# Sums over cached values with the values streamed: four heads in four 32-column parts of the array

## The reference, cut to what matters

```
def dilated_attn_decode(q, k_all, v_all, buf_len, dil, n_back):
    ...
    s = einsum('bshe,bsjhe->bhsj', q, kg) * ATT_SCALE
    p, lse = masked_softmax_lse(s, valid[None, None])
    o = einsum('bhsj,bsjhe->bshe', p, vg)         # sum over 129 places j
...
att = einsum('blhg,blhge->blhe', softmax(lses), outs)   # the three window groups merged
```

## Time and profile before

| what | value |
|---|---|
| median of 3 runs | 2080.9 us (2079.73 to 2081.86) |
| the profiled execution | 2077.44 us |
| its span, first to last instruction | 2075.6 us |
| PE busy | 2065.5 us (100%) |
| PEld busy | 2051.1 us (99%) |
| DVE busy | 1354.1 us (65%) |
| ACT busy | 1013.0 us (49%) |
| POOL busy | 478.0 us (23%) |
| granted TensorE clock | 9 or more tenths in all 40 slices |

### The profile page before, as it was taken

How to read it: one execution, slowest core, us unless ns; L and a number is a source line. 1 busy time by engine, 2 the same in 40 slices (tenths; PEclk the granted TensorE clock), 3 DMA queues, 4 the chain that set the end, 5 groups by cost and what they waited for, 6 DMA issues and landing times.

```text
span 2075.6 us, 48725 instructions
## 1 busy us (share of the span) xinstructions
PE 2065.5 (100%) x19202; PEld 2051.1 (99%) x19202; DVE 1354.1 (65%) x1441; ACT 1013.0 (49%) x1285; POOL 478.0 (23%) x526
## 2 busy tenths in 40 slices
PE   9999999999999999999999999999999999999999
PEld 9999999999999999999999999999999999999999
DVE  7567567775556767776759978665555555555555
ACT  6654344444444545653556675554443444434443
POOL 0686424420000206764307630110000000000000
PEclk9999999999999999999999999999999999999999
DMA  8987789987887788769969886578887888778874
GB/s 253 281 270 228 262 262 279 275 258 262 260 261 221 235 297 277 235 194 328 310 197 303 276 249 196 191 249 271 269 258 245 258 265 278 250 244 259 264 218 159
DMA packets 442478, 526.45 MB, mean 254 GB/s; under 512 B 41521, under 2 KB 423393, under 8 KB 439553
## 3 DMA queue, kind: packets, MB, share of 16 engines
q1 hardware_dynamic: 427184, 507.59, 77.8%
q0 software_dynamic: 3248, 11.62, 1.6%
q10 hardware_dynamic: 11936, 5.72, 1.1%
HBM read 506.75 MB, written 105.04 MB: 295 GB/s over the span
## 4 chain that ended last, share of the span: by engine, by line
PE 94%; DVE 2%; DMA 1%; issue 1%; ACT 1%; POOL 0%; SPq 0%; DVEq 0%; ACTq 0%; POOLq 0%
PE pa L1547 30%; PE pa L1548 30%; PE pa L1552 30%; DMA raw<-in_w_in 1%; DVE w_lo L1075 1%; ACT vu L892 0%; PE pb L1750 0%; DMA yt_v<-y_dram 0%; PE pb L1810 0%; PE pb L1788 0%; PE pb L1768 0%; DVE d_tmp L1353 0%; PE pb L1617 0%; PE pa L1904 0%; SPq L555 0%
## 5 line engine op out<-in xcount | busy, mean ns | idle before, releaser
L1075 DVE TENSOR_TENSOR w_lo<-raw,w_hi 128x1024 fp32r<-128x1024 f32 x735 | 939.3, 1291 | 508.0 <-ACT w_hi L660 503.5
L660 ACT ACTIVATE w_hi<-raw 128x1024 fp32r<-128x1024 f32 x735 | 766.4, 1053 | 647.2 <-PE pa L1552 548.3
L1547 PE MATMUL pa<-xg_hi,w_hi 128*128 128x264 f32 x3960 | 924.4, 278 | 0.0
L1548 PE MATMUL pa<-xg_lo,w_hi 128*128 128x264 f32 x3960 | 916.2, 276 | 0.0
L1547 PEld LDWEIGHTS pa<-xg_hi,w_hi 128*128 128x128 f32 x3960 | 748.4, 189 | 6.9 <-issue 4.8
L1548 PEld LDWEIGHTS pa<-xg_lo,w_hi 128*128 128x128 f32 x3960 | 748.6, 189 | 0.2
L1552 PE MATMUL pa<-xg_hi,w_lo 128*128 128x264 f32 x3960 | 526.4, 276 | 0.0
L1552 PEld LDWEIGHTS pa<-xg_hi,w_lo 128*128 128x128 f32 x3960 | 483.4, 189 | 0.0
L1547 PE MATMUL pa<-act_hi,w_hi 128*128 128x264 f32 x1632 | 378.4, 276 | 0.0
L1548 PE MATMUL pa<-act_lo,w_hi 128*128 128x264 f32 x1632 | 377.9, 276 | 0.0
L1548 PEld LDWEIGHTS pa<-act_lo,w_hi 128*128 128x128 f32 x1632 | 308.5, 189 | 0.0
(11 more groups left out here) (360 smaller groups left out, 1409.5 us busy)
## 6 DMA issues: line engine op xcount, KB each, us to landing
raw<-in_ffn_w_up SPq DMA_DIRECT2D x172, 512.0 KB, 5.5
raw<-in_ffn_w_gate SPq DMA_DIRECT2D x171, 512.0 KB, 4.9
out_kv_s<-in_cache_kv_w SPq DMA_DIRECT2D x165, 512.0 KB
raw<-in_ffn_w_down SPq DMA_DIRECT2D x160, 512.0 KB, 4.6
raw<-in_w_in SPq DMA_DIRECT2D x152, 512.0 KB, 5.5
raw<-in_w_out SPq DMA_DIRECT2D x32, 512.0 KB, 4.6
raw<-in_w_ssm_branch SPq DMA_DIRECT2D x16, 512.0 KB, 4.6
raw<-in_ffn_w_down SPq DMA_DIRECT2D x16, 384.0 KB, 4.0
```

The costliest lines, as they stand in the source:

```text
L660: act.activation(w_hi[:, slot], raw[:, slot], ACT.Copy).then_inc(hi_ready, 1)
L1075: dve.tensor_tensor(w_lo[:, slot], raw[:, slot], w_hi[:, slot].bitcast(f32), ALU.subtract).then_inc(lo_ready, 1)
L1547: pe.matmul(out, wh, in_order(hi), start=first, stop=False)
L1548: pe.matmul(out, wh, in_order(lo), start=False, stop=False)
```

## The change

The values now stream, and a small matrix stands as weights. `pick` holds, for each sample k, a block of 32 columns in which only column k is one. With it as weights, the product of a head's values (128 places x 128 features) comes out as 32 rows of 128 features, of which row k is the sum and the rest zero. The four heads go to the four 32-column parts of the array, so to four groups of 32 partitions of one PSUM tile. DVE adds these tiles over the samples into `v_acc` (128 x 128, in SBUF), PE turns `v_acc` once at the end (`turn_values`), and DVE adds the part of the new row for all samples at once (`values_out`). Because the sums moved from `pb` bank 0 to bank 2, which `y_products` also writes, the waits move too: `y_products(k)` waits for `add_values(k)`, and `value_sums(k)` waits for `read_y(k - 1)`. At the end `att_hi` waits for `values_out`, and `att_lo` moves from slab 5 to slab 7.

```
-    PV = YD + 2 * YW
+    PV = YS + 2 * YW
+    PT = PV + HD
...
-                        act.wait_ge(pv_read, NS)
+                        act.wait_ge(pv_read, NS + 1)
                         act.activation(halves(att_hi[:])[:, :, :, H1], by_parity(att_v[:, :, NT:T]), ACT.Copy).then_inc(att_hi_ready, 1)
...
+                    dstep(dve.memset(pick[:], 0.0))
+                    dstep(dve.memset(pick[:].rearrange("p s r -> p (s r)")[:, 0:32 * NS:33], 1.0))
...
             def add_values(k):
                 dve.wait_ge(pv_done, k + 1)
-                dve.tensor_tensor(att_v[:, :, bass.ds(NT + k, 1)], pb[:, 0, PV:PV + NSLOT, None],
-                                  att_new[:, 0, bass.ds(NSLOT * k, NSLOT), None], ALU.add).then_inc(pv_read, 1)
+                if below(k, 1):
+                    dve.tensor_copy(v_acc[:], pb[:, 2, PV:PV + HD]).then_inc(pv_read, 1)
+                else:
+                    dve.wait_ge(pv_read, k)
+                    dve.tensor_tensor(v_acc[:], v_acc[:], pb[:, 2, PV:PV + HD], ALU.add).then_inc(pv_read, 1)
+
+            def values_out():
+                dve.wait_ge(pv_done, NS + 1)
+                dve.tensor_tensor(att_v[:, :, NT:T], pb[:, 2, PT:PT + P].rearrange("p (h b) -> p h b", b=32)[:, :, 0:NS],
+                                  att_new[:, 0].rearrange("p (b h) -> p h b", h=NSLOT), ALU.add).then_inc(pv_read, 1)
...
-                if last:                                   # in state_turn_back, slab 5
-                    dve.wait_ge(att_hi_ready, 3)
-                    dve.tensor_tensor(halves(att_lo[:])[:, :, :, H1], ...).then_inc(att_lo_ready, 1)
...
+                    if at_end and j == 6:
+                        values_out()
+                    if at_end and j == 7:
+                        dve.wait_ge(att_hi_ready, 3)
+                        dve.tensor_tensor(halves(att_lo[:])[:, :, :, H1], ...).then_inc(att_lo_ready, 1)
...
             def y_products(k):
+                pe.wait_ge(pv_read, k + 1 if k < NS - 1 else NS + 1)
...
             def state_products(k):
-                    pe.wait_ge(pv_read, k)
...
             def value_sums(k):
                 pe.wait_ge(v_sum_ready, k + 1)
-                pe.wait_ge(sv_ready, 2 * k + 2)
+                if k:
+                    pe.wait_ge(y_read, k)
+                    pe.wait_ge(pv_read, k)
                 for hh in range(NSLOT):
-                    ins = pe.matmul(pb[:, 0, PV + hh:PV + hh + 1], vu[3 * (k % 2)][:, hh * HD:(hh + 1) * HD], ones[:, 0:1],
+                    ins = pe.matmul(pb[32 * hh:32 * hh + 32, 2, PV:PV + HD], pick[:, k, :], vu[3 * (k % 2)][:, hh * HD:(hh + 1) * HD],
                                     start=True, stop=True)
                 ins.then_inc(pv_done, 1)
+
+            def turn_values():                             # PE, last iteration, after slab 6
+                pe.wait_ge(pv_read, NS)
+                pe.transpose(pb[:, 2, PT:PT + P], v_acc[:], ident[:]).then_inc(pv_done, 1)
```

More of the change, by code:

```diff
@@ L248, in build_layer @@
     head_sd = tile("head_sd", [P, T], f32, RQ)
+    pick, v_acc = tiles(RQ, 8 * T, ("pick", [P, NS, 32]), ("v_acc", [P, HD]))
     head_r = tile("head_r", [P, 2, T], f32, RT + 24 * T)
@@ L1361, in state_turn_in, with state_turn_back @@
                 dve.tensor_tensor_scan(z_out[:, 0], M, z_in[:, 0], 0.0, ALU.mult, ALU.add).then_inc(scan_ready, 1)
-            def state_turn_back(k, h, last):
+            def state_turn_back(k, h):
                 E = tab[h][:, E0:M0].rearrange("p (a c) -> p a c", a=2)
@@ L1368, in state_turn_back @@
                 dve.tensor_tensor(d_tmp[:, 1], z_out[:, 1], E[:, 0], ALU.mult).then_inc(zi_step, 1)
-                if last:
-                    dve.wait_ge(att_hi_ready, 3)
-                    dve.tensor_tensor(halves(att_lo[:])[:, :, :, H1], by_parity(att_v[:, :, NT:T]),
-                                      halves(att_hi[:].bitcast(f32))[:, :, :, H1], ALU.subtract).then_inc(att_lo_ready, 1)
                 dve.wait_ge(zi_step, 5 * k + 5)
@@ L1389, in gates_b @@
                         state_turn_in(k, j // 4)
-                    last = at_end and j == 5
-                    if last:
+                    if at_end and j == 5:
                         add_values(NS - 1)
                     if j in ((2, 6) if opening else (1, 5)):
-                        state_turn_back(2 * i + j // 4, j // 4, last)
-                    if j in ((2, 6) if opening else (2, 5)) and not last:
+                        state_turn_back(2 * i + j // 4, j // 4)
+                    if j in ((2, 6) if opening else (2, 5)) and not (at_end and j == 5):
                         add_values(2 * i + j // 4)
+                    if at_end and j == 6:
+                        values_out()
+                    if at_end and j == 7:
+                        dve.wait_ge(att_hi_ready, 3)
+                        dve.tensor_tensor(halves(att_lo[:])[:, :, :, H1], by_parity(att_v[:, :, NT:T]),
+                                          halves(att_hi[:].bitcast(f32))[:, :, :, H1], ALU.subtract).then_inc(att_lo_ready, 1)
                     if opening and j == 0:
@@ L1893, in gates_b @@
                         value_sums(2 * i + j // 4)
+                    if i == ph.iters - 1 and j == 6:
+                        turn_values()
                     if j in ((1, 5) if i == 0 else (0, 4)):
```

2 lines of the change are left out of this document (1 added, 1 removed).

## The result

The changed kernel took 2084.05 us in the median (22 runs, 2080.97 to 2088.3), the kernel before 2079.73 us (22 runs on the same chip): ratio 1.0018, 95% interval 1.0013 to 1.0024. The forecast was 2083.9 us. Against these medians the change costs 4.3 us (2.7 to 5.0 by the interval of the ratio), where the forecast reckoned 3.0 on a median of before that was 1.2 us higher. The sign, the place and the order of size are as forecast; the terms are not all right.

What follows compares the result with a forecast made beforehand. In gates_b DVE and PE were both taken as full, each waiting for the other. 4.45 us at the end, less 1.0 and 0.85 given back, plus 0.3 before, made 3.0 on 2080.9: 2083.9 us, range 2079.8 to 2087.3.

Steps and rivals of the forecast that it cites:

- Value sums on PE: PE's value-sum block in gates_b: 0.90 to 0.55 us a sample, a gain of 2.8 us in all.
- Additions: DVE's add_values in gates_b: 0.28 us for 0.15, so 0.12 us more each, 1.0 us in all.
- Waits for bank 2: y_products and value_sums in gates_b: no gain up to slab 5 of the last iteration, 0.3 us lost on DVE's chain.
- DVE goes on without a gap: Reason given in gates_b, from 65.28 of 66 us busy, that PE can't get ahead of DVE.
- The wait before `y_products(6)`: In gates_b: the wait for add_values(6), 0.41 us, moves from state_products to y_products(6), whose 0.55 us no longer lies before it.
- The end: From add_values(7) through values_out, att_hi and att_lo: PE starts attn_branch at 1199.0, 4.45 us late, standing 3.6 us.
- Given back: Behind attn_branch's start: the later waits for L1475 (1.0 us) and for zs_lo (0.85 us) fall away.
- The sum: Whole kernel: 4.45 - 1.0 - 0.85 = 2.6 us, and 0.3 for DVE's chain before, in round 3.0 us slower.
- DVE moves with PE: Rival in gates_b: DVE looks full because PE and ACT pace it; -0.1 us, 2080.8 us, chance 0.15.
- Hidden end: Rival at slabs 5 to 7, last iteration: DVE reaches add_values(7) some 4.5 us earlier against PE; 2078.3 us, chance 0.04.
- Parts in series: Rival in the value sums: the four column parts run one after another, block 1.35 us; 2086.5 us, chance 0.08.
- The clock: Rival at the end of gates_b: PE's clock falls after its stalls, costing 3.3 us; 2087.2 us, chance 0.11.

Runs made afterwards that it cites:

- e10: The changed kernel with DVE's additions for samples 1 to 7 reading 4 columns in place of 128; 2083.12 us, before 2080.0, ratio 1.0016.
- e8: The kernel before with three of four heads' value sums left out for k = 1 to 7; 2081.23 us, before 2080.8, ratio 1.0.
- e1: The kernel before with only the two moved waits of y_products and value_sums added; 2080.09 us, before 2080.15, ratio 1.0003.
- e2: The kernel before with only att_lo moved from slab 5 to slab 7 of the last iteration; 2082.06 us, before 2080.15, ratio 1.0006.
- e3: The changed kernel with values_out at slab 5 and att_lo ahead of the last w_lo; 2080.11 us, before 2080.15, ratio 1.0001.
- e4: The changed kernel with every add_values(k) put ahead of state_turn_back(k) on DVE; 2082.59 us, before 2080.15, ratio 1.0014.
- e5: The changed kernel with every add_values(k) ahead of state_turn_back(k), and values_out and att_lo earlier at the end; 2080.17 us, before 2080.8, ratio 0.9999.
- e9: The kernel before with att_lo at slab 7 and extra one-column sums on PE before attn_branch; 2080.84 us, before 2080.0, ratio 1.0005.

## Why the prediction was right, point by point

- *Value sums on PE, 0.90 to 0.55 us.* Measured 0.56. The nearest row, L1750, and the reading that four column parts run side by side were good.
- *Additions, 0.12 us more each, 1.0 us in all.* The size was right (0.275 us where 0.28 was taken). That it adds up to 1.0 us is not borne out: with 0.9 us of it taken away, e10 is 0.15 us less late. For k = 0 to 2 DVE's additions stand at the same time from the marker as before, within 0.01 us, so there the longer addition delays nothing. The two memsets, 0.27 and 0.07 us, cost nothing either, as forecast: the slabs behind them keep their times. The Trainium skill's rule on PSUM ("TensorEngine Tiling (Array Packing)", "PSUM Bottleneck") is not shown at work here: no run shows a cost of the wider read from PSUM beyond the variation.
- *Waits for bank 2: no gain up to slab 5 of the last iteration, 0.3 us lost.* No gain: right, and e8 shows it apart from the change. The loss before the end is the mis-sized term: 1.70 us and not 0.3. Kernels with the old sums come there 0.09 to 1.14 us late, so up to 1.1 us of it can be variation between executions, and e1 shows that the waits alone are within it. Most of the 1.70 lies in steps that e2 has as well: 0.54 us up to k = 4 (e2 0.53) and 0.74 us behind the late load (e2 0.70). In the three kernels with the new sums and the old place of the additions (the change, e3, e10) it is 1.55 to 1.70, in the two with the additions ahead 0.39 and 0.80. That points to the additions' place, for the 0.4 to 0.6 us above the variation; with one execution of each it isn't shown, and the cause of that rest stays open.
- *"DVE goes on without a gap", 65.28 of 66 us.* The window of the earlier trace rows ends at 1169 us, and 1.8 us later DVE stands 1.46 us for `w_hi`. The same row has the DMA engines at 0.94, and the forecast gave the loads no price; the wait behind one of them grew by 0.74 us.
- *The wait before `y_products(6)`.* The forecast had the 0.41 us of the earlier trace rows and the saved 0.55 us move there, about 1 us. It was 2.50, since PE came sooner and DVE later. It cost nothing that the path shows, but the clock fell behind it (and behind 2.81 us in e3, not behind 2.60 in e10), and the forecast looked for that only at the end.
- *The end, 6.96 us from `add_values(7)` to PE.* Measured 6.56 (1195.80 to 1202.36), step for step on the same chain; `att_lo` beside an idle POOL takes 0.19 us and not the 0.63 of the earlier trace rows, L1387 beside a busy one 0.76 and not 0.5. `attn_branch` starts 4.06 us later than the chain before explains, forecast 4.45. PE's standing for it, 3.19 in the row, forecast 3.6. The stall for `turn_values` was 0.38 us and not 1.6: where the clock had fallen in slab 5, PE comes late (0.38 us in the change, 0.37 in e3), where it hadn't, the stall is as forecast (1.57 us in e4 and e5, 1.44 in e10).
- *Given back, 1.85 us.* Measured 2.14, by both waits named: PE waits neither before slab 2 of `attn_branch` nor in `glu` now. This holds while the clock does; where it fell at the end, 0.5 us came back.
- *The sum.* 1.70 + 4.06 - 2.14 = 3.62 us, forecast 0.3 + 4.45 - 1.85 = 2.9, said as 3.0. Three errors of 0.3 to 1.4 us, partly against each other: that 3.62 is near 3.0 is in part luck, since from the last scan on the cost was 1.92 us and not 2.6.
- *The level.* 2080.9 + 3.0 came out at 2083.9 by luck in part: before was 1.2 us lower in these runs, and the difference of the medians was 4.3.
- *Rivals.* DVE moves with PE: refuted (e8, and e5, where the saving is unspoilt and buys nothing). Hidden end: no, though narrowly; `add_values(7)` starts at 1195.80, and slab 6 ends at 1194.69 + 0.90 = 1195.59. Parts in series: no (0.43 us for eight records). The clock: it did fall, in every one of the 22 runs (mean clock 0.999 or 0.998, where before shows 1.0 in most); in the profiled one once, for 3.41 us, and where it costs nothing. Where it fell in the others the mean doesn't tell. Four runs at 0.998 take 2085.3 us in the mean and the 18 at 0.999 take 2083.9: in the four the end's stall probably lowered it as well, and a part of the 4.3 us between the medians may be that. Its price on the path was given as 3.3 us and is 1.65. With a chance of 0.11 it was held too cheap: of the five kernels whose PE stood 3 us or more before `attn_branch`, or did one-column work there, four show it in their profile. The two levels that the Trainium skill gives ("TensorE: Matmul & The Clock Gate", "What's actually happening") are those of the rows, 0.22 and 0.11 us between starts.

## What to carry to other kernels

Where two engines in fixed order are both full, find which one is waited for last before pricing a saving, and count the loads among them: here 2.7 us, and even 4.7 us, taken from the matrix engine bought nothing, while one small instruction moved behind two long ones on the other engine started the next phase 2.6 us later and cost 0.5 us with the clock held and 2.1 us with it lowered. When results that are collected step by step are finished "once at the end", the finishing chain (transpose, add, split in two) stands where nothing hides it: place each of its steps by hand ahead of the long work. A stall that costs nothing can still have a lowered clock of the matrix engine behind it: look at the granted clock behind each stall, and whether the slower stretch falls on the path.

## What the runs showed of the hardware that was not expected

- Each lowered stretch of the clock was 3.41 us long, in six kernels. In five it came after PE had stood 2.50, 2.81, 3.55, 3.19 or 3.32 us, 0.03 to 1.03 us after PE began again, in the sixth after the one-column sums of e9; it did not come after stalls of 3.19 us (the change, end) or 2.60 us (e10, `y_products(6)`). So the length of a stall alone doesn't decide it.
- 32 records of one streamed column, without idle time, did not hold the clock; 28 transposes of 128 columns did (one profiled execution each; mean clock below 1.0 in eight and two of 11 runs).
- Sums over partitions with the values streamed through four 32-column parts cost 0.56 us for four heads, against 0.90 us with the values as weights.
- A DVE copy of 128 x 8 took 0.69 us or 1.24 us beside POOL's work, ending 0.02 to 0.04 us after POOL's instruction each time, and 0.16 us without it; ACT did it in 0.22 us.
